# Inverse levels 1 to 5 on two diagonal 64x64 blocks, with Y turned by VectorE, in a hybrid decoder step

## What is computed

```python
a_mat = jnp.einsum('bhncd,bhnsd->bhncs', kb, k) * decay * strict
m_mat = jnp.eye(chunk, dtype=jnp.float32) + a_mat
rhs = jnp.concatenate([vb, kb * jnp.exp(gc)[..., None]], axis=-1)
sol = lax.linalg.triangular_solve(m_mat, rhs, left_side=True, lower=True, unit_diagonal=True)
u_c, w_c = sol[..., :DV], sol[..., DV:]
att = jnp.einsum('bhncd,bhnsd->bhncs', q, k) * decay
...
v_new = u_i - jnp.einsum('bhck,bhkv->bhcv', w_i, s)
o = (jnp.einsum('bhck,bhkv->bhcv', q_i * jnp.exp(gc_i)[..., None], s)
     + jnp.einsum('bhcs,bhsv->bhcv', att_i, v_new))
s = (s * jnp.exp(g_last)[..., None, None]
     + jnp.einsum('bhck,bhcv->bhkv', k_i * jnp.exp(g_last[..., None] - gc_i)[..., None], v_new))
```

## Time and profile before

| | |
|---|---|
| median of 3 runs | 1195.79 us (1195.64 to 1195.81) |
| the profiled execution | 1195.94 us |
| its span | 1194.2 us |
| TensorE busy in the span | 1181.5 us, 99% |
| VectorE busy | 790.0 us, 66% |
| ScalarE busy | 522.9 us, 44% |
| GpSimd busy | 63.3 us, 5% |
| TensorE clock granted | 0.999 of full |

### The profile page before, as it was taken

The page is one execution under the profiler, slowest core; times in us unless marked ns, Lnnn a source line. Parts: engine busy times, 40 slices in busy tenths (PEclk is TensorE's granted clock), DMA queues, the critical chain, the costliest instruction groups (busy, mean ns, idle before and its releaser), DMA issues.

```text
span 1194.2 us, 20994 instructions
## 1 busy us (share of the span) xinstructions
PE 1181.5 (99%) x8792; PEld 1157.0 (97%) x8792; DVE 790.0 (66%) x1153; ACT 522.9 (44%) x841; POOL 63.3 (5%) x48
## 2 busy tenths in 40 slices
PE   9999999999999999999999999999999999999997
PEld 9999999999999999999999898999999999999997
DVE  6887566767575743666567886537775767675764
ACT  6445333435334542433464444442443444354355
POOL 0000000000000300000014100220000000000003
PEclk9999999999999999999999999999999999999999
DMA  5422212222223322143300002322132121223122
GB/s 192 129 77 84 106 63 98 82 80 104 106 72 106 107 89 88 54 69 57 129 2 2 1 1 106 118 87 89 37 141 107 63 98 63 97 106 107 72 71 80
DMA packets 39213, 99.69 MB, mean 83 GB/s; under 512 B 12112, under 2 KB 15568, under 8 KB 39120
## 3 DMA queue, kind: packets, MB, share of 16 engines
q1 hardware_dynamic: 38064, 96.00, 24.6%
q10 hardware_dynamic: 1056, 2.36, 0.5%
HBM read 92.91 MB, written 5.44 MB: 82 GB/s over the span
## 4 chain that ended last, share of the span: by engine, by line
PE 95%; DVE 2%; ACT 1%; issue 1%; POOLq 0%; DVEq 0%; POOL 0%
PE ps L857 34%; PE ps L824 21%; PE ps L773 20%; PE ps L969 11%; PE ps L1362 4%; PE ps L737 1%; PE ps L1167 1%; PE ps L1376 1%; ACT x_hi L1444 1%; DVE w_lo L1951 1%; DVE h L2013 1%; PE ps L928 0%; PE ps L939 0%; PE ps L993 0%; PE ps L1273 0%
## 5 line engine op out<-in xcount | busy, mean ns | idle before, releaser
L857 PE MATMUL ps<-x_hi,s_hi 128*128 128x296 f32 (+1 forms) x576 | 171.4, 298 | 0.2
L857 PE MATMUL ps<-x_hi,s_lo 128*128 128x296 f32 (+1 forms) x576 | 170.9, 297 | 0.0
L857 PE MATMUL ps<-x_lo,s_hi 128*128 128x296 f32 (+1 forms) x576 | 170.6, 296 | 0.0
L773 PE MATMUL ps<-x_hi,w_hi 128*128 128x296 f32 (+1 forms) x608 | 135.7, 304 | 0.2 <-DVE x_lo L1956 0.2
L773 PE MATMUL ps<-x_lo,w_hi 128*128 128x296 f32 (+1 forms) x608 | 131.8, 298 | 0.0
L773 PE MATMUL ps<-x_hi,w_lo 128*128 128x296 f32 (+1 forms) x608 | 131.7, 298 | 0.0
L857 PE MATMUL ps<-t_hi,s_hi 128*128 128x296 f32 (+1 forms) x432 | 128.4, 297 | 0.0
L857 PE MATMUL ps<-t_hi,s_lo 128*128 128x296 f32 (+1 forms) x432 | 128.2, 297 | 0.0
L857 PE MATMUL ps<-t_lo,s_hi 128*128 128x296 f32 (+1 forms) x432 | 127.9, 296 | 0.0
L2050 DVE TENSOR_TENSOR s_lo<-s_sum,s_hi 128x1024 fp32r<-128x1024 f32 x72 | 88.2, 1225 | 44.5 <-ACT s_hi L1431 41.8
L857 PEld LDWEIGHTS ps<-x_hi,s_hi 128*128 128x128 f32 x576 | 108.4, 188 | 0.6 <-issue 0.6
(11 more groups left out here) (325 smaller groups left out, 2540.9 us busy)
## 6 DMA issues: line engine op xcount, KB each, us to landing
raw<-weights SPq DMA_DIRECT2D x150, 512.0 KB, 3.5
raw<-weights SPq DMA_DIRECT2D x16, 384.0 KB, 3.5
S<-states SPq DMA_DIRECT2D x1, 2048.0 KB, 10.7
new_state<-S ACTq DMA_DIRECT2D x1, 2048.0 KB, 6.8
y_t<-h SPq DMA_DIRECT2D x4, 336.0 KB, 2.3
h<-x_t SPq DMA_DIRECT2D x4, 296.0 KB, 4.8
h<-x_t SPq DMA_DIRECT2D x2, 592.0 KB, 7.8
raw<-weights SPq DMA_DIRECT2D x4, 256.0 KB, 5.2
```

Of the source, the lines that this page charges most:

```text
L773: last = nc.tensor.matmul(ps[:, slot if out is None else out, half, 0:w_half], w[:, slot, k, :], x[:, k, a:a + w_half], start=(k == 0 and ...
L857: last = nc.tensor.matmul(out, w[:, k, :], x[:, k, :], start=(start and k == 0 and r == 0), stop=(k == KT // 2 - 1 and r == 2), skip_group ...
```

## The change

For tiles 1 to 4, levels 0 to 5 work on the two diagonal 64x64 blocks of a tile alone. X, Y and T1 hold them packed, block 0 in partitions 0 to 63 and block 1 in partitions 64 to 127, each 64 columns wide (`x_small`, `y_small`, `t_small`). Each low and up product of a head becomes two 64x64 products, one for each block (`DIAGONAL`), into the two partition halves of the same 64 columns of one PSUM bank (`half_small`). VectorE's low and up operations are on 64 columns a head. After levels 0 to 4, where no block of Y is wider than 32, `flip` is one transpose on VectorE for two heads (it turns each 32x32 block in place); TensorE and ScalarE have no share in it. After level 5 TensorE transposes the first 64x64 block alone, and VectorE writes both blocks into the full inverse; level 6 writes its quarter without subtracting. Level 0 of the mask product is in two operations, and the quarter below the diagonal is set to zero once for each of the two buffers. Tile 0 and its 80x80 steps stay; the state products (d_egrow with S) stay as they are. The mask table is 128 columns narrower. ORDER is not changed.

```diff
@@ def turned / low / up / flip, TensorE
+                    else:
+                        r = DIAGONAL[0]
+                        last = nc.tensor.transpose(half_small(a + q, 0)[r, hd, :], inverse(t)[r, 2 * q + hd, r], ident[r, r])
...
                 pe.wait_ge(s["x_ready"][p][q], base + l)
+                if t and l == 1 and q == 1:
+                    if t == 1:
+                        pe.wait_ge(s["att_ready"], t + 1)
+                    elif t == 2:
+                        pe.wait_ge(s["y_ready"][0][1], LEVELS[0] - 1)
+                    else:
+                        pe.wait_ge(s["u_ready"], t - 2)
...
+                    elif t:
+                        for r in DIAGONAL:
+                            last = mm(half_small(a + q, 0)[r, hd - 2 * q, :], AT[p][r, hd, r], x_small(t)[r, hd, :])
...
+                    elif t:
+                        for r in DIAGONAL:
+                            last = mm(half_small(a + q, 1)[r, hd - 2 * q, :], t_small(t)[r, hd, :], y_small(t)[r, hd, :])
...
+                if t and l < 5:
+                    return
                 pe.wait_ge(s["y_ready"][p][q], base + l)
                 turned(t, q)
@@ def start / turned / flip / low / up, VectorE
+                if t:
+                    for r in DIAGONAL:
+                        last = V.tensor_tensor(t_small(t)[r], AT[p][r, :, r], small_mask(0)[r].unsqueeze(1).to_broadcast([HALF_P, H, HALF_P]),
+                                               ALU.mult)
+                    link(last)
...
+                if t == 1 or t == 2:
+                    V.memset(inverse(t)[HALF_P:P, :, 0:HALF_P], 0.0)
...
+            def turned(t, l, q):
+                p, a, b, base = chain_at(t)
+                if l == 0:
+                    dve.wait_ge(s["y_first"][p], t // 2 + 1)
+                else:
+                    dve.wait_ge(s["y_ready"][p][q], base + l)
+                V.transpose(two_heads(x_small(t), q), two_heads(y_small(t), q)).then_inc(s["x_ready"][p][q], 1)
+
+            def flip(t, lq):
+                if t and lq[0] < 5:
+                    turned(t, *lq)
...
+                elif t:
+                    V.tensor_tensor(two_heads(t_small(t), q), half_small(a + q, 0),
+                                    small_mask(l).unsqueeze(1).to_broadcast([P, 2, HALF_P]),
+                                    ALU.mult).then_inc(s["t1_ready"][p][q], 1)
...
-                    V.tensor_tensor(y, y, half_bank(a + q, 1, n)[0:HALF_P, :, HALF_P:P],
+                    V.tensor_scalar(y[0:HALF_P, :, HALF_P:P], half_bank(a + q, 1, n)[0:HALF_P, :, HALF_P:P], -1.0, None,
+                                    ALU.mult).then_inc(s["y_ready"][p][q], 1)
+                elif l == 5:
+                    for r in DIAGONAL:
+                        last = V.tensor_tensor(y[r, :, r], two_heads(y_small(t), q)[r], half_small(a + q, 1)[r], ALU.subtract)
+                    last.then_inc(s["y_ready"][p][q], 1)
+                elif t:
+                    V.tensor_tensor(two_heads(y_small(t), q), two_heads(y_small(t), q), half_small(a + q, 1),
                                     ALU.subtract).then_inc(s["y_ready"][p][q], 1)
```

More of the change, by code:

```diff
@@ L246 @@
 for _n, _w in (("ident", P), ("incl", P), ("neg", P), ("incl4", P), ("neg4", P), ("same4", P),
-               ("levels", 7 * P), ("group", NG)):
+               ("levels", 4 * MAIN), ("ident64", HALF_P), ("levels64", 6 * HALF_P), ("group", NG)):
     MASK[_n] = slice(_at, _at + _w)
@@ L265, in shape_masks @@
     m[:, MASK["same4"]] = same
-    for l in range(7):
+    for l in range(6):
         w = 1 << l
-        a = MASK["levels"].start + l * P
         block = (s // (2 * w) == c // (2 * w)) & (s % (2 * w) < w) & (c % (2 * w) >= w)
-        m[:, a:a + P] = block.T if l else block
+        block = block.T if l else block
+        if l < 4:
+            a = MASK["levels"].start + l * MAIN
+            m[:, a:a + MAIN] = block[:, 0:MAIN]
+        a = MASK["levels64"].start + l * HALF_P
+        for r in DIAGONAL:
+            m[r, a:a + HALF_P] = block[r, r]
+    m[:, MASK["ident64"]] = s % HALF_P == c[:, 0:HALF_P]
     m[:, MASK["group"]] = seq[:, None] == np.arange(NG)[None, :]
@@ L485, in half_bank, with half_small, x_small, y_small @@
             return bank(j).rearrange("p (x h c) -> p x h c", x=2, h=2)[0:n, half, :, 0:n]
+        def half_small(j, half):
+            return bank(j).rearrange("p (x h c) -> p x h c", x=2, h=2)[:, half, :, 0:HALF_P]
+        def x_small(t):
+            return XY[t % 2][:, 0, :, 0:HALF_P]
+        def y_small(t):
+            return XY[t % 2][:, 0, :, HALF_P:P]
+        def t_small(t):
+            return T1[t % 2][:, :, 0:HALF_P]
+        def two_heads(ap, q):
+            return ap[:, 2 * q:2 * q + 2]
+        def first_mask(l):
+            a = MASK["levels"].start + l * MAIN
+            return mask[0:MAIN, a:a + MAIN]
+        def small_mask(l):
+            a = MASK["levels64"].start + l * HALF_P
+            return mask[:, a:a + HALF_P]
         def side_banks(t):
@@ L1781, in start @@
                 p, a, b, base = chain_at(t)
-                if i == 1:
+                if i == 1 and t == 0:
                     for q in range(2):
@@ L2459, in start @@
                 if i:
+                    if t:
+                        for q in range(2):
+                            turned(t, 0, q)
                     return
@@ L2608, in nothing @@
                 pass
-            steps = {"prep": prep, "tok": tok, "start": start, "low": low, "up": up, "flip": nothing, "end": end, "scan": scan, "first": first, "states": nothing,
+            steps = {"prep": prep, "tok": tok, "start": start, "low": low, "up": up, "flip": flip, "end": end, "scan": scan, "first": first, "states": nothing,
                      "silu": silu, "cast": cast, "heads": lambda t, i: x_heads(t), "weights": weights_split, "store": nothing}
```

40 lines of the change are left out of this document (24 added, 16 removed).

## The result

The change gained nothing: 1198.86 us median of 15 runs (1193.72 to 1205.3), against 1195.78 for the kernel before (15 runs, 1195.42 to 1197.4). The ratio is 1.0028, 95% interval 1.0015 to 1.0041: slower by 0.3%, outside the range that was forecast. Its runs also lie 11.6 us apart, where those of before lie 2 apart, and they order themselves by TensorE's mean granted clock: 0.995 at 1193.7, 0.990 at 1198.7, 0.983 at 1205.3. The profiled execution is one of the fastest: 1194.02 us, span 1192.2.

The account below looks back on a forecast made before the run. TensorE was taken to bound the inverses' stretch, VectorE next; with 88.0 and 91.7 us of work left, the middle saving of 13.1 us gave 1195.94 - 13.1 - 0.15 = 1182.7 us, range 1175.6 to 1191.6.

Parts of the forecast that it names:

- What bounds before: Stretch building the inverses, 112.47 us: TensorE, busy 110.75 us, is the bound; VectorE, 88.43, is next to bind.
- Side by side: Low and up steps: a head's two diagonal 64x64 blocks overlap on TensorE, 0.23 us a step, 18.6 us for 80.
- The rival of one bank: Both blocks write one PSUM bank, so passes alternate; TensorE gains only 4.2 us, 1191.6 us in all; chance 0.14.
- The transpose's price: VectorE's 40 new 128x128 transposes cost 0.29 us each, 11.6 us; VectorE's work in the stretch becomes 91.7 us.
- TensorE's 88.0 us: TensorE's work left in the inverses' stretch after 22.7 us less from smaller products and dropped transposes, net of size changes.
- Together: TensorE's 88.0 and VectorE's 91.7 us share the inverses' stretch: between 6.2 and 20.0 us saved, middle 13.1.
- the second rival: Turns of Y wait in VectorE's queue, 0.57 us of idle TensorE for each of 40: 1195.6 us, no change; chance 0.06.

Follow-up runs that it names:

- The kernel with the blocks alone: The changed kernel with its turns of Y left to TensorE (64x64 identity products) and ScalarE's copy, not VectorE: 1196.2 us, ratio 1.0002.
- the turns alone: The kernel before, products still 128x128, with Y turned by VectorE after levels 0 to 4: 1203.73 us, ratio 1.0062.
- The pair of kernels with the long wait: The kernel before with VectorE making tile 2's first Y four times: 1206.15 us; the same with 24 products of ones in that wait: 1200.85 us.
- filler at one place: The changed kernel, turns right behind updates, ScalarE copying U, 4 full-width products of ones ahead of level 1 of tile 2: 1191.14 us.
- filler at five places: The changed kernel, turns right behind updates, ScalarE copying U, 12 full-width products of ones at five places: 1191.01 us, ratio 0.9962.
- the turns forward: The changed kernel with VectorE's turns of levels 1 to 4 right behind the updates of Y: 1195.07 us, ratio 0.9994.
- the turns forward and U on ScalarE: The changed kernel with turns right behind updates, level 0's right behind the first Y, and U copied by ScalarE: 1194.13 us, ratio 0.999.
- filler at five places with the turns in place: The changed kernel, turns where the change has them, with 12 full-width products of ones at five places: 1196.39 us, ratio 1.0007.

## Why the prediction was wrong

- **What bounds before**: right. TensorE's work could shrink, and VectorE was next.
- **Side by side**: right. A step takes 0.23 to 0.28 us, and the two blocks' passes start within 0.01 us; one after the other it would take twice the 0.23. The rival of one bank is out, and with it the rule in the Trainium skill, TensorEngine Tiling, Restrictions and Gotchas, as far as it would forbid this: outputs in different partitions of one bank go on together.
- **The transpose's price**: right, 0.291 us for 0.29. VectorE is busy 88.8 us in the stretch, not 91.7; where the difference lies was not followed up. The Trainium skill's rule in the Vector Engine (DVE) Microarchitecture Reference, section 3.8, agrees: a turn (0.291) costs what an operation of its size does (0.283).
- **TensorE's 88.0 us**: it is 95.4. Up to 3.4 of the 7.4 us are the clock (6.8 us at half speed). The other 4.0 I can't assign; busy rows run to a modelled end, and there are many more short runs that end in a wait.
- **Together** is the step that failed. It took the middle of 6.2 and 20.0 us saved, and neither end held: the stretch is 1.5 us shorter. It argued only from the engines' busy sums, fifth by fifth. Its lower bound assumed that the share of idle time in VectorE's fullest fifth would carry over. But a turn is on the chain from every update to the next low product, and the unchanged order puts other operations ahead of it: 11 waits, 10.3 us. That was the second rival (given 0.06), in fewer and longer waits than its 0.57 us for each of 40. Its argument against, that the way through TensorE and ScalarE falls away, was true and too small. The kernel with the blocks alone is as fast at the same clock, so the turns' waits ate what the transposes had given; with the turns alone they cost more than that. One of the 11 waits, the 1.37 us, has another cause besides the queue: an operation of VectorE ahead of that turn took 1.32 us longer than elsewhere, beside GpSimd's work (see the last section).
- **The granted clock** was in no step: a term put at nothing without a reason. It stood in the earlier trace rows as 1.00 in each fifth, and I took it for a constant, where it depends on TensorE being kept busy. In the profiled execution it cost up to 3.4 us. The median run stands 4.8 us above that one with a clock 0.005 lower, and a line through the 15 runs falls 0.89 us for each 0.001 of clock. Carried on, beyond the 0.995 that any run reached, to the 0.998 to 0.999 of the kernel before it gives 1191.6 to 1190.7, an estimate: a gain of 4 to 5 us, which the clock takes back, with 3 more. The median is 16.2 us over the forecast; by this estimate about half of that is the clock, and the other half the step Together. The Trainium skill, TensorE: Matmul & The Clock Gate, Part 1, says that the clock follows how busy the engine has been lately, and that the place of the change differs between runs of one kernel. The pair of kernels with the long wait agrees with the first (0.992 and 0.998). The second fits mean clocks from 0.983 to 0.995 in runs of one kernel, but each kernel has one trace, so no run here shows the places. The forecast should have weighed it.

What stays open: why the runs of one kernel differ so much in mean clock, and whether idle time or thin work (small products) counts more ahead of a fall. The fall with the blocks alone, behind 2.04 us of idle TensorE in one piece, suggests idle time. The trace with filler at one place speaks for thin work: its clock falls at 638.1 us, and in the 8 us before that TensorE waited once, for 0.68 us. With filler at five places the same wait stands there, four passes of ones follow it, and the clock holds:

```profile
635.65 0.51 PE L1002 MATMUL ps<-d_inv,d_a_t 80*80 80x80 f32 x4 [0.68 <-ACT d_inv L1846]
636.85 0.69 PE L1002 MATMUL ps<-ones 128*128 128x128 f32 x4
```

One trace of each can't settle it, since their runs vary; no run separates the two.

## What to carry to other kernels

Where an engine is 99% busy, take work off it only as fast as the next engine can hand over results: move a step that is on the chain to another engine's queue together with its place in that queue, and read what stands ahead of it there. Treat the granted clock as a result of the schedule, not as a given: a single new wait of some 2 us on TensorE cost more than as much again behind it (2.04 us, and 4.7 us gained by filling it), and a spread of runs that follows the clock is its sign. A few full-width products of no use inside such a wait are then cheap, and here they turned no gain into 0.3%; put everywhere they cost what they give.

## What was not expected of the hardware

- One wait of 5.80 us on TensorE was followed by half speed up to 662.7 us, 10.3 us after work had resumed at 652.4, though TensorE was busy 4.00 of every 4.00 us from 653 to 661.
- 64x64 products ahead of 16 steps did not keep the clock up (0.988 to 0.997 over 12 runs), while 8 products of 128x128 in the one wait of another kernel did (0.998 in six of nine runs).
- VectorE's turn takes 0.291 us for 128x128 and 0.425 for 128x256, about as the mask products of the same sizes (0.283 and 0.42).
- Two 64x64 blocks on the diagonal share a PSUM bank and still start their passes within 0.01 us of each other.
- In tile 2's start the subtraction that makes the first Y took 1.75 us, where those of the other three tiles take 0.42 to 0.43. GpSimd's product of 80x1024 (L2792) ran beside it, and it is this operation that TensorE's wait of 1.37 us hangs on. In the run with the longer wait three such operations of 128x512 took 5.30 us beside the same products of GpSimd, and the fourth, begun after those had ended, 0.69. The kept traces say more. In five of them (the changed kernel, the blocks with and without filler, the turns forward, filler at five places with the turns in place) the subtraction begins 0.42 to 0.43 us behind the start of GpSimd's product, takes 1.75 us, and ends 0.3 us behind that product's end; with the turns forward and U on ScalarE it begins 0.23 behind, takes 1.95 and ends 0.3 behind it too. In the kernel before, and with the turns alone, it begins 0.09 us ahead of GpSimd's product, and it is GpSimd that takes longer: 2.35 us against 1.90 for its next product. So it looks as if whichever begins second gives way, while VectorE's operations that read PSUM are hardly touched: four of L2476 take 1.11 us beside GpSimd's next product, and 1.08 at two places without GpSimd. A shift of half a microsecond in the order turned this cost on, and with it most of the wait that stands ahead of the first fall of the clock. No run takes GpSimd's product away to prove it. The kernel before:

```profile
646.31 0.69 DVE L2471 TENSOR_TENSOR d_inv<-mask,d_t 128x512 f32<-128x512 f32 x1
646.40 2.35 POOL L2703 TENSOR_TENSOR work<-d_v_new,mask 80x1024 f32<-80x1024 f32 x1 [1.56 <-ACT d_v_new L1841]
```

The Trainium skill, GPSIMD Engine Reference, section 1 (Specifications), has GpSimd share its SBUF interfaces with VectorE, with contention for VectorE instructions that have two SBUF inputs. The subtraction has two, and the durations agree. The changed kernel, GpSimd and VectorE in order of time:

```profile
646.29 1.90 POOL L2792 TENSOR_TENSOR work<-d_v_new,mask 80x1024 f32<-80x1024 f32 x1 [1.74 <-ACT d_v_new L1893]
646.71 1.75 DVE L2535 TENSOR_TENSOR d_inv<-mask,d_t 128x256 f32<-128x256 f32 x1
```
